# A decoder layer on one core: pooling products kept in SBUF, an emptying step put between the next pair's steps, and the sample chunk first in the FFN's end

## The reference, cut to what matters

```python
h = rmsnorm(x, g_mix) * (1 + sc1) + sh1
z = h @ w_in
u, q, k, v, o, ig, fg, gp, gm = jnp.split(z, IN_SPLITS, axis=-1)
y_pool, new_hist = pool_mixer(u, pool_hist, pos0, w_pool, s_pool)
hm, C1, n1, m1 = mlstm_mixer(qf, kf, vf, igf, lff, C0, n0, m0)
hm = hm * lax.rsqrt(jnp.mean(hm * hm, axis=-1, keepdims=True) + EPS)
y_ml = (hm.reshape(B, T, ML_WIDTH) * g_head.astype(f32)).astype(x.dtype) * jax.nn.sigmoid(o)
merged = jax.nn.sigmoid(gp) * (y_pool @ w_bp) + jax.nn.sigmoid(gm) * (y_ml @ w_bm)
x = x + gt1 * (merged @ w_out)
h2 = rmsnorm(x, g_ffn) * (1 + sc2) + sh2
gate, up = jnp.split(h2 @ w_gu, 2, axis=-1)
x = x + gt2 * ((jax.nn.silu(gate) * up) @ w_down)
```

## Time and profile before

| | |
|---|---|
| runs of the kernel before | 2094.68 us median of 3 (2093.05 to 2095.66) |
| the profiled execution: its own time, its span | 2094.26 us, 2092.5 us |
| PE busy; PEld; DVE; ACT; POOL | 1992.2 us; 1892.3; 770.2; 472.4; 188.5 |
| chain that ended last | PE 90%, DVE 4%, DMA 2%, ACT 2% |
| granted clock of PE, mean of the run | 0.979 |
| moved by DMA | 209.75 MB, 100 GB/s over the span |

### The profile page before, as it was taken

One profiled execution on the slowest core, in us unless ns is written; L12 is line 12 of the kernel. 1 busy time (PEld: TensorE's weight loads), 2 busy tenths in 40 slices (PEclk: granted clock), 3 DMA queues, 4 the chain that ended last, 5 costly groups with the idle time before them and its releaser, 6 DMA issues.

```text
span 2092.5 us, 28618 instructions
## 1 busy us (share of the span) xinstructions
PE 1992.2 (95%) x11631; PEld 1892.3 (90%) x11631; DVE 770.2 (37%) x1323; ACT 472.4 (23%) x673; POOL 188.5 (9%) x267
## 2 busy tenths in 40 slices
PE   7699999999999999999899987999999999999997
PEld 3499998999999997777899986999999999999996
DVE  2732221222333333223534447323432442343236
ACT  2333222222434432212112012111111111111113
POOL 3401007301000002130000003000000000000000
PEclk9899999999999999999999988999999999999998
DMA  7545334452243347453753220111111111111112
GB/s 248 190 133 165 120 121 124 142 152 82 88 122 97 88 130 162 148 172 136 233 181 111 83 61 20 42 41 50 40 49 41 40 50 40 40 50 40 41 50 86
DMA packets 227377, 209.75 MB, mean 100 GB/s; under 512 B 13411, under 2 KB 202647, under 8 KB 227311
## 3 DMA queue, kind: packets, MB, share of 16 engines
q1 hardware_dynamic: 218190, 175.23, 28.2%
q10 hardware_dynamic: 7721, 29.25, 3.5%
q0 software_dynamic: 1408, 4.46, 0.7%
HBM read 154.65 MB, written 54.37 MB: 100 GB/s over the span
## 4 chain that ended last, share of the span: by engine, by line
PE 90%; DVE 4%; DMA 2%; ACT 2%; issue 1%; SPq 0%; ACTq 0%; DVEq 0%
PE dense L1702 77%; PE misc L1988 2%; DMA z_scratch<-stage 1%; PE misc L1791 1%; PE misc L1975 1%; PE misc L1914 1%; PE misc L1918 1%; PE misc L1887 1%; DVE stage L1194 1%; PE misc L1916 1%; PE misc L1816 1%; PE misc L1815 1%; DVE stage L1195 1%; DVE act_lo L1201 0%; PE misc L2084 0%
## 5 line engine op out<-in xcount | busy, mean ns | idle before, releaser
L1702 PE MATMUL dense<-act_hi,w_hi 128*128 128x384 f32 (+1 forms) x2808 | 648.2, 339 | 36.7 <-DVE act_lo L1201 25.8
L1702 PE MATMUL dense<-act_lo,w_hi 128*128 128x384 f32 (+1 forms) x2808 | 623.7, 330 | 0.0
L1702 PE MATMUL dense<-act_hi,w_lo 128*128 128x384 f32 (+1 forms) x2808 | 622.6, 330 | 0.0
L1702 PEld LDWEIGHTS dense<-act_hi,w_hi 128*128 128x128 f32 x2808 | 482.9, 190 | 61.7 <-issue 36.4
L1702 PEld LDWEIGHTS dense<-act_hi,w_lo 128*128 128x128 f32 x2808 | 483.7, 189 | 0.0
L1702 PEld LDWEIGHTS dense<-act_lo,w_hi 128*128 128x128 f32 x2808 | 483.5, 189 | 0.0
L1186 DVE TENSOR_TENSOR w_lo<-raw,w_hi 128x1024 fp32r<-128x1024 f32 x139 | 176.9, 1273 | 471.3 <-ACT w_hi L824 470.6
L824 ACT ACTIVATE w_hi<-raw 128x1024 fp32r<-128x1024 f32 x139 | 147.0, 1058 | 406.8 <-PE dense L1702 366.9
L1633 DVE SCALAR_TENSOR_TENSOR hmT<-dense,mod,hmT 128x768 f32<-128x768 f32 x80 | 81.4, 1018 | 69.0 <-PE dense L1702 68.6
L916 ACT ACTIVATE stage<-dense 128x768 f32<-128x768 f32 x52 | 42.2, 812 | 284.8 <-PE dense L1702 284.6
L1702 PE MATMUL dense<-a_lo,w_hi 128*128 128x384 f32 (+1 forms) x480 | 106.3, 329 | 0.0
(11 more groups left out here) (293 smaller groups left out, 1562.4 us busy)
## 6 DMA issues: line engine op xcount, KB each, us to landing
z_scratch<-stage ACTq DMA_DIRECT2D x52, 544.0 KB, 2.7
raw<-in_w_in_dram SPq DMA_DIRECT2D x53, 512.0 KB, 3.8
ada_w<-in_w_ada_dram SPq DMA_DIRECT2D x24, 1024.0 KB, 5.2
raw<-in_w_gate_up_dram SPq DMA_DIRECT2D x44, 512.0 KB, 3.7
stage<-z_scratch SPq DMA_DIRECT2D x24, 544.0 KB, 3.7
raw<-in_w_down_dram SPq DMA_DIRECT2D x22, 512.0 KB, 3.5
oin<-z_scratch SPq DMA_DIRECT2D x16, 544.0 KB, 5.0
qkv<-z_scratch SPq DMA_DIRECT2D x8, 1024.0 KB, 6.8
```

The lines of the kernel that those rows point to most:

```text
L1702: ins = pe.matmul(tile(k, c), w[:, n % 2, off:off + P], x[:, xr, t0:t1], start=(first and p == 0), stop=(last and p == 2))
```

## The change

Three parts. (1) In the chunk stage the first pass is written out ahead of the loop, and in every later one the last unit of the pass before is emptied by `l2_step(-1, ...)` between the steps of the first unit, as it is done for the others. (2) DVE writes the pooling products into a new SBUF tensor `share`, which overlies wpool, d012 and the sample states; the stores and the loads back go, the gate rows are loaded by `rows_in` (which waits until the tile two before is free), the store of n moves to the end, and the merge multiplies into a new `prod`. Before the product of unit 3 DVE waits for the last states' stores. `oin` and d3 lie a few columns further on. (3) In the last FFN pass a32, a_hi and a_lo of the second hidden block are made chunk by chunk in the order sample chunk, first, second; PE does the first block's passes of three outputs before any of the second; the chunks of the down product follow the same order, and with them the finished row tiles (`Y_ORDER`); `y_turn` and `y_rows` stand one output earlier in a chunk. In the part left out of the diff the same indices j and tt are renamed in the rest of `last_down`, `y_turn`, `y_rows` and the final stores.

```diff
+LAST_CH = (2, 0, 1)
+Y_ORDER = (6, 7, 8, 0, 1, 2, 3, 4, 5)
...
-        sb(yps, "over_cs0_cs1", [P, 4584])
+        sb(yps, "over_cs0_cs1_kb", [P, 4928])
         oin = sb(yps, "oin", [P, 2, T])
-        sb(yps, "over_kb_to_hs", [P, 1424])
+        prod = sb(yps, "prod", [P, T])
         d3 = sb(yps, "d3", [P, T])
         yps.close()
+        merge = ExitStack()
+        share = sb(merge, "share", [P, KT, T])
+        merge.close()
...
-
-                wait_full(sp, tile_free, T_BP + j)
-                sp.dma_start(z[Z_GP + j], stage[:, j % 2, :]).then_inc(stage_out[j % 2], 16)
+            def rows_in(k, src, i=0, per=0):
+
+                wait_free(sp, tile_free, k, i, per)
+                sp.dma_start(stage[:, k % 2, :], src).then_inc(gin_in[k % 2], 16)
 
             gm_load(0)
             head_rows(0, 0)
...
 
+            for s in range(2):
+                sp.wait_ge(stage_out[s], 26 * 16)
             for j in range(2):
-                gp_in(j)
+                rows_in(T_BP + j, z[Z_GP + j])
                 sp.dma_start(oin[:, j, :], z[Z_O + j]).then_inc(oin_in[j], 16)
-            wait_full(sp, round_free, R_NOUT)
-            sp.dma_start(n_s[0].rearrange("b h d -> (b h) d"), nout[:, :]).then_inc(outs, 16)
             for j in range(KT):
                 if j % 2 == 0:
                     u = U_BP + 2 + j // 2
                     load(u, *((bp_src(u), 0, 0, PG) if u < U_BM else (w_cols(w_bm[0], P * (u - U_BM)),)))
-                share_out(j)
                 if j + 2 < KT:
-                    gp_in(j + 2)
+                    rows_in(T_BP + j + 2, z[Z_GP + j + 2])
                     sp.wait_ge(yml32_ready, j + 1)
                     sp.dma_start(oin[:, j % 2, :], z[Z_O + j + 2]).then_inc(oin_in[j % 2], 16)
-
-            def rows_in(k, src, i=0, per=0):
-
-                wait_free(sp, tile_free, k, i, per)
-                sp.dma_start(stage[:, k % 2, :], src).then_inc(gin_in[k % 2], 16)
-
...
             for j in range(KT):
                 rows_in(T_BM + j, z[Z_GM + j])
-                if j < 2:
...
-                    store(k, zrow(i * 2 + (Z_O + KT * (j // 2) + j % 2)), i, 4)
+                    store(k, zrow(i * 2 + (Z_GP - 1 if j < 0 else Z_O + KT * (j // 2) + j % 2)), i, 4)
 
             def gm_step(m, i=0, per=0):
...
-            def l2_act(i, last=False):
+            def l2_act(i, first=False, last=False):
                 for j in range(4):
                     if j == 2:
                         weights(1, i)
                     for s in range(8):
                         chunk_act(j // 2, i, (j % 2) * 8 + s)
-                        if j:
+                        if j or not first:
                             l2_step(j - 1, i, s)
-                if last:
-                    return
-                weights(0, i + 1)
-                for s in range(4):
-                    l2_step(3, i, s)
+                if not last:
+                    weights(0, i + 1)
 
             weights(0, 0)
-            with act.Fori(0, NCK // 2 - 1) as i:
+            l2_act(0, first=True)
+            with act.Fori(1, NCK // 2 - 1) as i:
                 l2_act(i)
             l2_act(NCK // 2 - 1, last=True)
...
-                    act.wait_ge(a32_ready, i * 2 + (f + 2))
-                    act.activation(a_hi[:, f, :], a32[:, f, :], ACT.Copy).then_inc(ahi_ready, 1)
+                    if last and f:
+                        for j, c in enumerate(LAST_CH):
+                            t0, t1 = CH[c]
+                            act.wait_ge(la32_ready, j + 1)
+                            act.activation(a_hi[:, f, t0:t1], a32[:, f, t0:t1], ACT.Copy).then_inc(lahi_ready, 1)
+                    else:
+                        act.wait_ge(a32_ready, i * 2 + (f + 2))
+                        act.activation(a_hi[:, f, :], a32[:, f, :], ACT.Copy).then_inc(ahi_ready, 1)
                     split_hi(n + 2 * f + 2, i, 6)
                 if last:
...
+                if j == PG - 1:
+                    dve.wait_ge(cs_out[1], 2 * NB * 16)
+                gated(T_BP + j, share[:, j, :])
                 y = hmT[:, j, :]
...
-                gated(k, sq[:, :], i, 2)
+                gated(k, prod[:, :], i, 2)
                 wait_full(dve, tile_free, k, i, 2)
                 if between is not None:
                     between()
-                wait_full(dve, oin_in, KT + j, i, 2, 16)
-                dve.tensor_tensor(m, oin[:, j, :], sq[:, :], ALU.add).then_inc(m32_ready, 1)
+                dve.tensor_tensor(m, row(share, kt), prod[:, :], ALU.add).then_inc(m32_ready, 1)
                 if between is None:
                     split_lo(U_BM + 2 + j, i, 2)
...
+                    if last and f:
+                        for j in range(len(CH) + 1):
+                            if j < len(CH):
+                                t0, t1 = CH[LAST_CH[j]]
+                                dve.tensor_tensor(a32[:, f, t0:t1], tile(t, LAST_CH[j]), sil[:, t0:t1], ALU.mult
+                                                  ).then_inc(la32_ready, 1)
+                            if j:
+                                t0, t1 = CH[LAST_CH[j - 1]]
+                                dve.wait_ge(lahi_ready, j)
+                                dve.tensor_tensor(a_lo[:, f, t0:t1], a32[:, f, t0:t1], a_hi[:, f, t0:t1].bitcast(F32),
+                                                  ALU.subtract).then_inc(la_ready, 1)
+                        split_lo(n + 2 * f + 2, i, 6)
+                        return
                     dve.tensor_tensor(wide(a32[:, f, :]), tile_wide(t), wide(sil[:, :]), ALU.mult)
                     dve.tensor_tensor(a32[:, f, 768:T], tile(t, 2), sil[:, 768:T], ALU.mult).then_inc(a32_ready, 1)
                     dve.wait_ge(ahi_ready, i * 2 + (f + 1))
                     dve.tensor_tensor(a_lo[:, f, :], a32[:, f, :], a_hi[:, f, :].bitcast(F32), ALU.subtract
                                       ).then_inc(tile_free[t % 2], 1)
                     split_lo(n + 2 * f + 2, i, 6)
...
-                    dve.scalar_tensor_tensor(out=ytok[0:rows, tt % 4, n0:n0 + 512], in0=y_banks(tt, rows)[:, half, :],
...
-            last_down(1, 6)
-            y_rows(2)
-            last_down(2, 0, 4)
-            y_rows(3)
-            last_down(2, 4, 6)
-            y_rows(4)
-            last_down(2, 6)
-            for tt in range(5, TT):
-                y_rows(tt)
+            for j in (1, 2):
+                last_down(j, 0, 3)
+                y_rows(3 * j - 3)
+                last_down(j, 3, 5)
+                y_rows(3 * j - 2)
+                last_down(j, 5, 7)
+                y_rows(3 * j - 1)
+                last_down(j, 7)
+            for j in range(6, TT):
+                y_rows(j)
 
 
         @block.tensor
...
+            def last_pass(j, o, f):
+
+                c = LAST_CH[j]
                 t0, t1 = CH[c]
-                n = U_FFN + 6 * FI - 2
-                for o in range(lo, hi):
-                    m = KT * c + o
-                    if c == 0 and o % 4 == 0:
-                        halves(n + o // 4)
+                n = U_FFN + 6 * FI - 2 + o // 4
+                m = KT * j + o
+                if j == 0 and o % 4 == 0 and f == 0:
+                    halves(n)
+                if f == 0:
                     if m == 0:
                         wait_full(pe, tile_free, T_DOWN_LAST - 2)
+                    elif m == LAST_BANKS - 1:
+                        pe.wait_ge(la32_ready, len(CH))
                     elif m >= LAST_BANKS:
                         pe.wait_ge(x2_ready, KT * (FI - 1) + m + 1 - LAST_BANKS)
+                elif o == 0:
+                    pe.wait_ge(la_ready, j + 1)
+                for p in range(3):
+                    w, x = ((w_hi, a_hi), (w_hi, a_lo), (w_lo, a_hi))[p]
+                    off = 512 * f + P * (o % 4)
+                    ins = pe.matmul(last_bank(m, 0, t1 - t0), w[:, n % 2, off:off + P], x[:, f, t0:t1],
+                                    start=(f == 0 and p == 0), stop=(f == 1 and p == 2))
...
+                ins.then_inc(y_full[j % 2], 1)
+
+            for f in range(2):
+                for o in range(LAST_BANKS - 1):
+                    last_pass(0, o, f)
+            last_down(0, LAST_BANKS - 1)
+            for j in (1, 2):
+                last_down(j, 0, 2)
+                y_turn(3 * j - 3)
+                last_down(j, 2, 4)
+                y_turn(3 * j - 2)
+                last_down(j, 4, 6)
+                y_turn(3 * j - 1)
+                last_down(j, 6)
+            for j in range(6, TT):
+                y_turn(j)
 
 
 # ---- launch: one core; inputs and outputs as the reference has them ----
```

More of the change, by code:

```diff
@@ L359, in last_bank, with y_banks @@
             return (dense[:, 3, lo:hi], misc[:, 0, lo:hi], misc[:, 1, lo:hi], dense[:, 2, lo:hi])[j]
-        def y_banks(tt, rows):
-            b = 4 * (tt % 2)
+        def y_banks(j, rows):
+            b = 4 * (j % 2)
             return dense[0:rows, b:b + 2, :]
@@ L656, in _ @@
```

(53 more changed lines are left out.)

45 lines of the change are left out of this document (14 added, 31 removed).

## The result

| | before | changed |
|---|---|---|
| median of 4 runs | 2093.86 us | 2071.31 us (2067.27 to 2073.20) |
| ratio | | 0.9891, 95% interval 0.9872 to 0.9911 |
| profiled execution: own time, span | 2094.26, 2092.5 us | 2071.99, 2070.2 us |
| mean granted clock | 0.979 | 0.980 |
| moved by DMA | 209.75 MB | 200.84 MB |

The account below looks back on a forecast made before the run. PE, busy 95% of the span, bounds the kernel; only its stops and slow clock can pay. 7.7 + 10.4 + 0.0 = 18.1 us off 2094.26 gives 2076.2, with the median 0.4 higher 2076.6 us; range 2072.5 to 2083.

Parts of the forecast that it names:

- Part 1, -7.7: Chunk stage: with the last unit emptied between steps, even chunks become as short as odd ones, saving 7.7 us.
- rival D: Chunk stage: a table switch costs double, 1.28 us more in three even chunks, total 2080.4 us; chance 0.02.
- Part 2, -10.4: Pooling to mLSTM projection: products in SBUF let the second unit's weights come earlier and shorten PE's stops, saving 10.4 us.
- B: Pooling stage: row loads slip 7 us, weights stay late, PE stops 3.3 us; total 2081.4 us; chance 0.10.
- E: Pooling stage: row loads become PE's bound, slower than before, 2103 us if landing takes 15 us; chance 0.03.
- Part 3, 0.0: FFN's end: thirds and the new chunk order bring no net gain, bounds -2.5 and +2.5 us.
- I take the fall: FFN's end: PE's clock falls behind a new stop of 1.9 us, turning a gain of 2.0 into 0.0.
- The walk at full clock, -2.0: FFN's end if the clock holds: -1.4 us by sum, -2.1 by engine walk, -2.0 taken; as a rival, chance 0.25.
- The first term: FFN's end: PE is through the first chunk at 2052.1 instead of 2055.0, -2.9 us.
- The second: FFN's end: two chunks of 8.3 us with six transposed tiles replace 8.3, 7.05 and five tiles, +2.2 us.
- The third: FFN's end: DVE's lag behind PE goes from 3.8 to 2.1 us, costing 1.0 at the chunk change, -0.7.
- Tail: Behind the last update: the same three tiles and a store of 512 instead of 256 KB, no change, 0.

Follow-up runs that it names:

- the last version: Changed kernel with the last w_hi and w_lo early, turned tiles one output later, mLSTM second unit's w_lo ahead of act_lo of row 3: 2067.84 us, ratio 0.9876.
- part 3 alone: The kernel before with only the edit of the FFN's end: 2087.8 us, ratio 0.9980.
- late turning: The changed kernel with turned tiles and their rows one output later in a chunk, as before the change: ratio 0.9883.
- the moved load: The kernel before, with the weights of the mLSTM projection's second unit asked for on SP right behind those of the first: 2091.72 us, ratio 0.9999.
- part 2 alone: The kernel before with only the pooling products kept in SBUF: 2082.16 us, ratio 0.9952.
- part 1 alone: The kernel before with only the last unit emptied between steps in the chunk stage: 2084.78 us against 2092.24, ratio 0.9962.
- the stores kept: The kernel before with the products in SBUF, but SP still writing the eight product stores in their old place: 2084.1 us, ratio 0.9951.

## Why the prediction was right or wrong

**What bounds the kernel: right.** Only stops of PE and the clock behind them moved.

**Part 1, -7.7: right,** -7.5 in the changed kernel and -7.6 alone. Taking odd chunks as the model for even ones was sound: from the second on all are 37.2 us apart. The size leans on the execution before, in which the clock fell at both boundaries (last section). The table load between the kw pairs took 1.28 us, and the tile's first ACTIVATE started 0.01 us behind it (565.97, then 567.26), so rival D falls. The rule of the Trainium skill's page ScalarE: Activation LUTs (What ACT_TABLE_LOAD costs), that a drain comes on top of the load, does not hold here.

**Part 2, -10.4: right in size,** -10.5. (The stretch takes 268.1 to 269.8 us in the four kernels with the old stage, and 259.1 to 260.1 in all with the new one but the last version, which has 258.2.) The queue ran as walked: weights asked for at 1016.46, which is 6.8 us less than the forecast 1023.3 in a kernel that was 7.0 us ahead by then; stop 0.62 against 0.5; clock 1.00. The reason given was half the truth. "Its weights were asked for at 1035.84 and took 7.38 us, because SP's queue first waited for the products' stores" named one of two chains, and with only that one mended nothing is gained. The other ran through the last gate row, for which DVE waited 3.83 us. The change mended both, and the walk through the new kernel had that row in it, so the number held although the cause named for the old stop was incomplete. Rivals B and E fall: no row was late.

**Part 3, 0.0: wrong,** -4.8: 3.65 us in the FFN's end and 1.15 in the tail. The steps that failed:

- "I take the fall": wrong, 2.0 us. The stop of 1.65 us came at its place, and in all four executions that have it (the changed kernel twice, part 3 alone, late turning) the clock stayed at 1.00. The choice was drawn from one stop of 1.92 us with a fall and one of 1.8 us without, and does not hold (last section).
- The walk at full clock, -2.0: short by 1.65 us. The written sum was -2.9 + 2.2 - 0.7 = -1.4; the same three terms measured -3.0, +1.3 and -1.95, together -3.65. By taking -2.0 instead, the prediction had made good 0.6 us of the difference. The first term was right: PE was through the first chunk 9.35 us after DVE's first product; 9.3 was forecast. The second, "two chunks of 8.3 us with six transposed tiles", was 0.9 too high: the old length was counted as 20.2 us where the trace of before shows 20.8 (2055.12 to 2075.96), and the new one as 22.4 where it is 22.2 (2034.62 to 0.17 us behind the start of the last pass, 2056.61). The third was 1.25 too small: DVE's lag behind PE at the end went from 3.8 to 1.8 us (2.1 was forecast), and the 1.0 "at the change of chunk" did not come; PE's pause there is 0.17 us (2047.67 to 2047.84), already in the 22.2.
- "Tail: the same three tiles behind the last update ...: 0": wrong, 1.15 us. Before, it was the rows of four tiles and not of three, since those of tile 5 (1.4 us) came behind the last update too and held a pair of banks from a tile that waited to be turned. But most of the 1.15 is the clock. With the old FFN's end the tail takes 12.75 to 12.77 us in the three executions in which the clock fell behind its stop of 2.8 us, and 11.96 and 11.93 in the two in which it fell only later; with the changed one it takes 11.59 to 11.65 in four executions, and 12.19 in part 3 alone, where the last turned tile ran at half clock. So 0.8 us is that fall, and 0.3 is left for the order.

These are 2.0 + 1.65 + 1.15 = 4.8 us, all in one direction, and the range's low end had only 2.5 us for this part and nothing for the tail. The start of the run lost 0.6 us, so that the profiled execution lies 4.2 below its forecast of 2076.2. The median lies 1.1 further below: it was taken to be 0.4 above the profiled execution and is 0.7 under it.

## What to carry to other kernels

When a stop ends with one late thing, follow the other inputs of the same instruction and of those queued ahead of it on its engine too: two chains of nearly equal length look like one, and mending the one that ended last buys the difference alone. Where a buffer is stored and loaded again, count the turn (store, completion, load) and not the bytes. At the end of a program, put work that nobody waits for behind the last producer on its engine, not ahead of it, and read the old length of a stretch from the trace instead of building it from rates. Before a gain is put down to an edit, see in both profiles whether the clock fell in that stretch: of the 4.8 us of part 3, 2.4 are falls that came in one execution and not in the other.

## What the runs showed of the hardware that was not expected

The same stop at the same place does not always bring the same clock. Two stops of 1.92 us in one execution, the first and second boundary of the chunk stage in the kernel with the moved load (us, PE busy (x), PEclk, DMA share, GB/s):

```profile
569.00:572.00 3.00, 3.00 (x16) 0.60 0.00 0
646.60:649.60 3.00, 3.00 (x20) 1.00 0.00 0
```

A stop of 1.80 to 1.85 us in the sample states, at the third head, which the change doesn't touch: the kernel before held its clock behind it, part 2 alone did not. (The window of the earlier trace rows for this stop, 887.60 to 889.60, lies within it; this is the one behind it.)

```profile
890.70:893.70 3.00, 3.00 (x15) 1.00 1.07 367
```

```profile
891.50:894.50 3.00, 3.00 (x10) 0.59 1.06 368
```

Of the 13 profiled executions, 8 take 173.8 to 173.9 us from the first product of the sample states to the first of the pooling stage, and 5 take 175.5 to 175.6: 1.7 us is what a fall costs there. The stop of 3.44 us in the FFN's end of before was followed by a fall in the kernel before and in those with part 1 alone, part 2 alone and the stores kept, where the FFN's end took 36.98 to 37.95 us, and by none in the kernel with the moved load, where it took 35.40:

```profile
2038.70:2042.70 4.00, 3.97 (x12) 0.50 0.00 0
```

```profile
2045.80:2049.80 4.00, 4.00 (x23) 1.00 0.00 0
```

(the first is part 2 alone, the second the moved load). So from 1.8 to 3.4 us of stop, the fall is a matter of chance as far as these traces tell, at 0.8 (in the tail) to 2.5 us a time; what decides it stays open. The kernel before has several such stops, and its runs spread from 2086.6 to 2098.3 us over the experiments. The gain read from the two profiles holds three such falls. At a clock of 1.00 in both, the FFN's end gains 35.40 - 33.34 = 2.1 us and not 3.65, and the tail 0.3 and not 1.15. And the old chunk stage took 306.1 to 306.2 us in the three executions in which the clock fell at both boundaries, but 304.3 and 304.5 in the two in which it held at the second: against these part 1 would have gained 5.8 us and not 7.5.

The Trainium skill's page TensorE: Matmul & The Clock Gate (HAM oscillation) warns of idle gaps longer than the 1.92 and 1.85 us behind which the rows above show falls; there the measurement decides. Its remark (Part 1), made of a kernel's start, that one and the same kernel has different numbers of slow matmuls from run to run agrees with them.
